# Expert rows added straight into the output by indirect DMA, in place of a combining stage

## The chip, the cores and the metric

The kernel runs on one core of one Trainium2 chip. The metric is the device time of one execution, in microseconds (us). Before the change the median of three runs is 3893.79 us (3890.04 to 3899.09). The profile is that of one execution more.

## The reference, cut to what matters

One layer of a decoder for 2048 prompt rows and 64 sample rows of width 1024. After two attention sublayers every row goes through a mixture of experts: a router picks two of 32 gated-MLP experts for it, and the weighted outputs of both are added to the row.

```python
def moe_ffn(xf, ids, wts, w_gate, w_up, w_down):
    ...
    xb = xf[row_tok].reshape(n_blocks, MOE_BLOCK, -1)      # MOE_BLOCK = 128
    def expert_block(args):
        xblk, e = args
        return (jax.nn.silu(xblk @ w_gate[e]) * (xblk @ w_up[e])) @ w_down[e]
    yb = lax.map(expert_block, (xb, blk_e)).reshape(rows, -1).astype(F32) * row_w[:, None]
    return jnp.zeros(xf.shape, F32).at[row_tok].add(yb).astype(xf.dtype)
# layer: h = h + MemCrossAttn(RMSNorm(h), mem);  y = h + HierMoE(RMSNorm(h))
```

## The kernel before, in words

The program is a list of stages (`STAGES`), one after the other; each ends with a barrier of all engines (`Stage.__exit__`). Inside a stage each engine has its own instruction queue, written out by hand, and semaphores order them. Four stages matter here.

**Memory attention** (`attend_memory`, L2507) walks over 17 tiles of 128 rows. SP stores the residual rows of a tile (`h2_store`, L2581) to the scratch tensor `h2`, and the normalised rows (`hn_store`) to `hn`.

**Routing** (`route`, L2784): DVE works out for each row its two experts, weights and places, in a list sorted by expert and padded to blocks of 128. Then POOL scatters the row numbers into the list `i_rows` (L2847): 34 indirect DMAs of 128 rows of 4 bytes. SP saves the places (`i_dst`), the weights and a plan: for each block its expert, the number of experts begun so far, and whether it begins a new one.

**Experts** (`experts`, L2945) loops over the blocks, two to a loop turn (`blocks`, L2980). The trace has 48 used blocks and 32 loads of each weight; the gate loads are some 19 us apart where an expert has one block and some 36.5 us where it has two: 16 experts of each kind. Each engine runs its `work` for block b:

- SP loads gate and up weights (2 MiB each) when a block begins a new expert.
- POOL waits until the rows of block b have been transposed, gathers the rows of block b+2 (`gather`, L3037, an indirect DMA of 128 rows of 4 KiB), loads the down weights (2 MiB) of block b+1 if that begins an expert, once DVE has split the down weights before them (`d_split`), waits for the gathered rows to land, and loads the row numbers of block b+4 (L3031).
- ACT takes the upper part of each weight (L3076), the SiLU, and copies the result of a block from PSUM to `ex_y` (L3107); it then stores `ex_y` to its place in the scratch tensor `yb` (L3109).
- DVE makes the lower part of each weight (L3130), splits the transposed rows (`ex_xT`, `ex_hT`) and multiplies (`ex_hh`).
- PE does three float32r products for each matmul (L136 to L138): up of block b, transposition of block b+2, gate of block b+1, down of block b.
- When the loop of SP is past the used blocks it stores zeros to the 18 unused blocks of `yb` (L3018).

**Combining** (`combine`, L3214): for each of 17 tiles, SP loads the `h2` rows, POOL gathers the two expert rows of each row from `yb` (L3254), DVE multiplies each by its weight and adds (L3264, L3269), SP stores the sum to `y` (L3231).

Of the kernel before, what the change touches and what calls it, by code (L numbers as in the profile page):

```python
# [53 lines left out]
NBX = NBLK + 4  # L54
# [2452 lines left out]
def attend_memory(nc, t, wo):  # L2507
# [6 lines left out]
    with Stage(nc, "mx") as s:  # L2514
# [27 lines left out]
                 "ox_turned oxT_hi oxT_ok xo_mm h1_in h2_ok ss_ok mean_ok root_ok rstd_ok h0_ok hn_ok h_turned hT_ok lg_mm lg_ok h2_out hn_out lg_out").split()  # L2542
# [16 lines left out]
        with nc.Block() as block:  # L2559
            @block.sync  # L2560
            def _(sp):
# [30 lines left out]
                sp.dma_start(wr[:], t["w_r"].rearrange("(k p) c -> p k c", p=P)).then_inc(E["w_in"], 16)  # L2592
                order(sp, lambda i: each((prompt(q_load), i + 1), (h1_load, i - 1), (h2_store, i - 2), (hn_store, i - 2),
                                         (sample_rows, i - 1), (lg_store, i - 3)))
                for e in ("h2_out", "hn_out", "lg_out"):
                    sp.wait_ge(E[e], NT * 16)

# [186 lines left out]
def route(nc, t):  # L2784
# [6 lines left out]
    with Stage(nc, "rt") as s:  # L2791
# [5 lines left out]
        tok = s.sb("tok", [P, NT], I32)  # L2797
        valid = s.sb("valid", [P, NT])
        zero = s.sb("zero", [P, NBX], I32)
# [21 lines left out]
        names = "loaded zero_ok zeroed own exp_ok sums_ok placed planned scattered saved".split()  # L2821
# [3 lines left out]
        with nc.Block() as block:  # L2825
            @block.sync
            def _(sp):
                sp.dma_start(lg[:], t["lg"].rearrange("n p c -> p n c")).then_inc(E["loaded"], 16)
                for dstt, name in ((io, "r_iota"), (kb, "r_blocks"), (ib, "r_places"), (tri, "r_tri"), (tok, "r_tok"), (valid, "r_valid")):
                    sp.dma_start(dstt[:], t[name]).then_inc(E["loaded"], 16)  # L2830
                sp.wait_ge(E["zero_ok"], 1)
                sp.dma_start(t["i_rows"].rearrange("(p n) o -> p (n o)", p=P), zero[:]).then_inc(E["zeroed"], 16)
                sp.wait_ge(E["placed"], 1)
                sp.wait_ge(E["planned"], 1)
                for dd, src in ((t["i_dst"], dsti[:]), (t["wts"], wts[:]), (t["i_plan"], plan[0:1])):
                    sp.dma_start(dd, src).then_inc(E["saved"], 16)
                sp.wait_ge(E["saved"], 48)

            @block.gpsimd
            def _(pool):  # L2840
                pool.memset(zero[:], 0).then_inc(E["zero_ok"], 1)
                pool.wait_ge(E["zeroed"], 16)
# [26 lines left out]
            def _(dve):  # L2869
# [75 lines left out]
def experts(nc, t):  # L2945
# [6 lines left out]
    with Stage(nc, "ex") as s:  # L2952
        ident = s.sb("ident", [P, P])
        plan = s.sb("plan", [1, 3, NBX + 1], I32)
        idx = s.sb("idx", [P, 2, 1], I32)
# [8 lines left out]
        zero = s.sb("zero", [P, D])  # L2964
# [5 lines left out]
                 "gate_mm up_mm sg_ok hh_ok h_turned h_hi h_ok y_mm y_ok y_out0 y_out1 zero_ok zero_out").split()  # L2970
# [9 lines left out]
        def blocks(eng, body, beyond=None):  # L2980

            used = read(eng, 0, NBX, NBLK)
            with eng.Fori(0, NBLK // 2) as i:
# [3 lines left out]
                if beyond:  # L2987
                    with eng.If(2 * i >= used):
                        for u in range(2):
                            beyond(2 * i + u)  # L2990
# [10 lines left out]
        with nc.Block() as block:  # L3001
            @block.sync
            def _(sp):
# [4 lines left out]
                def load(i, u, b):  # L3008
                    sp.sem_inc(E["zero_out"], 16)
# [10 lines left out]
                sp.wait_ge(E["zero_ok"], 1)  # L3020
                blocks(sp, load, nothing)
                sp.wait_ge(E["zero_out"], 16 * NBLK)

            @block.gpsimd
            def _(pool):
                pool.memset(zero[:], 0.0).then_inc(E["zero_ok"], 1)
# [6 lines left out]
                def gather(u, b, nth):  # L3033
# [3 lines left out]
                    pool.indirect_dma_start(xb[:, u, :], None, t["hn"].rearrange("n p d -> (n p) d"),  # L3037
                                            bass.IndirectOffsetOnAxis(ap=idx[:, u, :].bitcast(U32), axis=0)).then_inc(E[f"x_in{u}"], 16)
# [6 lines left out]
                for u in range(2):  # L3045
                    gather(u, u, 1)
# [3 lines left out]

                load_down(read(pool, 0, 0, NE - 1))

                def work(i, u, b):
                    pool.wait_ge(E["x_turned"], b + 1)
                    gather(u, b + 2, i + 2)
# [5 lines left out]
                    pool.wait_ge(E[f"x_in{u}"], 16 * i + 32)  # L3061
                    pool.sem_inc(E["seen"], 1)
                    load_rows(u, b + 4)

                pairs = blocks(pool, work)
                for u in range(2):
                    pool.wait_ge(E[f"idx_in{u}"], 16 * pairs + 32)

            @block.scalar
            def _(act):  # L3070
# [18 lines left out]
                def work(i, u, b):  # L3089
# [22 lines left out]
                for u in range(2):  # L3112
                    act.wait_ge(E[f"y_out{u}"], 16 * pairs + 16)
                    act.sem_inc(E["seen"], 1)

            @block.vector
            def _(dve):
# [5 lines left out]
                dve.sem_inc(E["y_out0"], 16)  # L3123
                dve.sem_inc(E["y_out1"], 16)
# [89 lines left out]
def combine(nc, t):  # L3214
    with Stage(nc, "cb") as s:
# [225 lines left out]
```

## Time and profile before

| | us |
|---|---|
| median of three runs | 3893.79 |
| the profiled execution | 3893.31 |
| its span in the trace | 3891.7 |
| PE busy over the span | 3223.6 (83%) |
| POOL busy over the span | 398.2 (10%) |

The span is what the trace covers; 1.6 us of the profiled execution's own time lie around it. Engines: PE is TensorE, DVE VectorE, ACT ScalarE, POOL GpSimd, SP the sync engine; a name with q is an engine's queue. A row of the timeline gives start, length, engine, line, operation, what is written and read, and in brackets how long the engine was idle before and what released it. "To landing" runs from the issue of a DMA until its data are there.

### The profile page before, as it was taken

Reading aid. Unit: us, or ns where it says so; the run is one execution under the profiler, and the core shown is the slowest. Engines: PE = TensorE matmul, PEld = TensorE weight load, DVE = VectorE, ACT = ScalarE, POOL = GpSimd, SP = SyncE. Lnnn points to the kernel's source line nnn. Section 1 sums busy time; section 2 is a strip of 40 time slices with the busy share of each in tenths; the row PEclk is TensorE's granted clock in tenths of the full one; section 3 lists DMA queues with packets and bytes.
Section 4 is the critical chain, followed back from the end, with each engine's and each line's share of the span. In section 5 each row is a group of like instructions: output and inputs, shape, how many; then the busy total and the mean of one; then the engine's idle time right before and its main releaser. Section 6 shows DMA issues by size and latency. Waiting matters only on the chain. (4 is left out here: it accounts for less than half of the span.)

```text
span 3891.7 us, 62377 instructions
## 1 busy us (share of the span) xinstructions
PE 3223.6 (83%) x22582; PEld 2700.3 (69%) x22583; DVE 1889.6 (49%) x2769; ACT 1486.6 (38%) x2958; POOL 398.2 (10%) x393
## 2 busy tenths in 40 slices
PE   7999999899969996568599966888339999999980
PEld 7999999788858885334277743677237778778860
DVE  5242356455534555311256631332436876686734
ACT  5112354355545554123123212443035655454520
POOL 1000000000000000040000010111131211121113
PEclk9999999899979998678699986988569999999995
DMA  4333332234441111164233322223158977796849
GB/s 163 121 110 140 140 110 99 86 115 127 148 127 35 64 56 51 51 200 135 98 117 114 115 95 89 90 95 98 37 193 305 340 283 269 273 350 228 293 180 340
DMA packets 309939, 591.64 MB, mean 152 GB/s; under 512 B 80597, under 2 KB 136323, under 8 KB 309230
## 3 DMA queue, kind: packets, MB, share of 16 engines
q1 hardware_dynamic: 250846, 365.54, 28.6%
q0 software_dynamic: 47776, 196.29, 13.7%
q10 hardware_dynamic: 11136, 27.27, 1.9%
q8 instruction: 130, 2.13, 0.2%
q14 instruction: 51, 0.42, 0.0%
HBM read 462.13 MB, written 160.44 MB: 160 GB/s over the span
## 5 line engine op out<-in xcount | busy, mean ns | idle before, releaser
L136 PE MATMUL pj_pu<-pj_w,pj_nT 128*128 128x256 f32 (+3 forms) x1088 | 306.8, 282 | 0.0
L137 PE MATMUL pj_pu<-pj_w,pj_nT 128*128 128x256 f32 (+3 forms) x1088 | 305.9, 281 | 0.0
L138 PE MATMUL pj_pu<-pj_w,pj_nT 128*128 128x256 f32 (+3 forms) x1088 | 305.2, 281 | 0.0
L137 PEld LDWEIGHTS pj_pu<-pj_w,pj_nT 128*128 128x128 f32 (+1 forms) x1088 | 202.1, 186 | 0.0
L138 PEld LDWEIGHTS pj_pu<-pj_w,pj_nT 128*128 128x128 f32 (+1 forms) x1088 | 202.0, 186 | 0.0
L136 PEld LDWEIGHTS pj_pu<-pj_w,pj_nT 128*128 128x128 f32 (+1 forms) x1088 | 201.6, 185 | 0.1
L3076 ACT ACTIVATE ex_gate<-ex_gate_raw 128x2048 fp32r<-128x2048 f32 x64 | 119.1, 1909 | 204.0 <-DMA ex_gate_raw<-in_w_gate 116.8
L716 ACT ACTIVATE att_prob<-att_score,att_res 128x256 f32<-128x256 f32 (+1 forms) x384 | 127.6, 443 | 143.9 <-DVE att_res L752 143.9
L3130 DVE TENSOR_TENSOR ex_gate<-ex_gate_raw,ex_gate 128x2048 fp32r<-128x2048 f32 x64 | 143.8, 2288 | 72.1 <-ACT ex_gate L3076 60.9
L136 PE MATMUL pj_pu<-pj_nT,pj_w 128*128 128x384 f32 (+2 forms) x480 | 175.3, 365 | 0.0
L136 PE MATMUL ex_py<-ex_down,ex_hT 128*128 128x512 f32 x384 | 152.7, 398 | 26.2 <-DVE ex_hT L131 26.2
L138 PE MATMUL pj_pu<-pj_nT,pj_w 128*128 128x384 f32 (+2 forms) x480 | 170.2, 355 | 0.0
L758 DVE COPY att_pT<-att_turn 128x512 f32<-128x512 f32 (+1 forms) x192 | 107.2, 572 | 129.9 <-PE att_turn L812 129.4
L137 PE MATMUL pj_pu<-pj_nT,pj_w 128*128 128x384 f32 (+2 forms) x480 | 169.9, 354 | 0.0
L136 PE MATMUL ex_gu<-ex_gate,ex_xT 128*128 128x512 f32 x392 | 162.9, 416 | 0.4 <-DVE ex_gate L3130 0.4
L826 PE MATMUL att_outp<-att_va,att_pT 128*128 128x65 f32 x1200 | 160.5, 271 | 0.3 <-DVE att_pT L758 0.3
L3130 DVE TENSOR_TENSOR ex_up<-ex_up_raw,ex_up 128x2048 fp32r<-128x2048 f32 x64 | 143.8, 2288 | 28.7 <-issue 22.7
L826 PEld LDWEIGHTS att_outp<-att_va,att_pT 128*128 128x128 f32 x1200 | 148.9, 191 | 11.7 <-issue 8.0
L138 PE MATMUL ex_gu<-ex_gate,ex_xT 128*128 128x512 f32 x392 | 154.4, 394 | 0.0
L137 PE MATMUL ex_gu<-ex_gate,ex_xT 128*128 128x512 f32 x392 | 153.7, 392 | 0.0
L3130 DVE TENSOR_TENSOR ex_down<-ex_down_raw,ex_down 128x2048 fp32r<-128x2048 f32 x64 | 143.7, 2287 | 15.5 <-issue 10.7
L138 PE MATMUL ex_py<-ex_down,ex_hT 128*128 128x512 f32 x384 | 149.7, 390 | 0.0
(580 smaller groups left out, 8168.6 us busy)
## 6 DMA issues: line engine op xcount, KB each, us to landing
ex_gate_raw<-in_w_gate SPq DMA_DIRECT2D x32, 2048.0 KB
ex_up_raw<-in_w_up SPq DMA_DIRECT2D x32, 2048.0 KB, 11.2
ex_down_raw<-in_w_down POOLq DMA_DIRECT2D x32, 2048.0 KB, 8.4
tmp_yb<-ex_y ACTq DMA_DIRECT2D x48, 512.0 KB, 7.1
out_win_k<-in_cache_k POOLq DMA_DIRECT2D x8, 2032.0 KB, 13.1
out_win_v<-in_cache_v POOLq DMA_DIRECT2D x8, 2032.0 KB, 14.2
tmp_att<-att_res POOLq DMA_DIRECT2D x48, 264.0 KB, 4.4
pout_att<-tmp_att SPq DMA_DIRECT2D x16, 792.0 KB, 7.4
```

Of the source, the lines that this page charges most:

```text
L136: pe.matmul(out, ah, bh, start=start, stop=False)
L137: pe.matmul(out, ah, bl, start=False, stop=False)
L138: return pe.matmul(out, al, bh, start=False, stop=stop)
L716: e = act.activation(prob[:, b % 2, h, lo:], score[:, place(h), lo:], ACT.Exp, bias=res[:, b % RES, AH * VA + h:AH * VA + h + 1])
L758: dve.tensor_copy(pT[:, j, 0:n, :], turn[:, j % 2, 0:n * P].rearrange("p (c n) -> p c n", c=n)).then_inc(p_moved, 1)
L826: last = pe.matmul(outp[:, j // 2, (2 * (j % 2) + h) * VA:(2 * (j % 2) + h + 1) * VA], pT[:, j, h * halves + k, :], va[:, slot, 2 * j + h, :],
L3076: act.activation(half[p][:, 0, part(p, h)], raw[p][:, part(p, h)], ACT.Copy).then_inc(E[p + "_hi"], 1)
L3130: dve.tensor_tensor(half[p][:, 1, part(p, h)], raw[p][:, part(p, h)], half[p][:, 0, part(p, h)].bitcast(F32), ALU.subtract).then_inc(E[p + ...
```

## The change

Memory attention stores its residual rows into the output `y` itself; `h2`, `yb`, `i_dst` and the saved weights are gone. The list `i_rows` now holds pairs (row number, weight), padded with rows of an extra tile at the end of `hn` and `y` (the former padding was row 0), which memory attention fills once. The experts' ACT multiplies by the weight in the copy from PSUM. POOL then adds the 128 rows of `ex_y` to their rows of `y` by an indirect DMA with an add, and waits until that has landed before it goes on. Gathers run three blocks ahead instead of two. ACT's store to `yb`, the zeros, and the whole combining stage are taken out.

```diff
-NBX = NBLK + 4
+NBX = NBLK + 8
...
-                    sp.dma_start(t["h2"][i], h2[:]).then_inc(E["h2_out"], 16)
+                    sp.dma_start(t["y"][i], h2[:]).then_inc(E["h2_out"], 16)
...
+                sp.wait_ge(E["consts_in"], 80)
+                for n in ("hn", "y"):
+                    sp.dma_start(t[n][NT], gf[:]).then_inc(E["spare_out"], 16)
...
-        tok = s.sb("tok", [P, NT], I32)
+        tokw = s.sb("tokw", [P, 2, NT, 2], I32)
...
+                sp.dma_start(t["i_rows"].rearrange("(p n) o -> p (n o)", p=P), t["r_fill"]).then_inc(E["filled"], 16)
...
-                for dd, src in ((t["i_dst"], dsti[:]), (t["wts"], wts[:]), (t["i_plan"], plan[0:1])):
-                    sp.dma_start(dd, src).then_inc(E["saved"], 16)
-                sp.wait_ge(E["saved"], 48)
+                sp.dma_start(t["i_plan"], plan[0:1]).then_inc(E["saved"], 16)
+                sp.wait_ge(E["saved"], 16)
 
...
-                                                tok[0:n, i:i + 1], None).then_inc(E["scattered"], 16)
+                                                tokw[0:n, a, i, :], None).then_inc(E["scattered"], 16)
...
+                own.then(dve.tensor_copy(tokw[:, :, :, 1].bitcast(F32), wts[:]))
...
-        idx = s.sb("idx", [P, 2, 1], I32)
+        idx = s.sb("idx", [P, 2, 2], I32)
+        place = s.sb("place", [P, 2, 2], I32)
...
-                def nothing(b):
-                    sp.dma_start(t["yb"][b], zero[:]).then_inc(E["zero_out"], 16)
-
-                sp.wait_ge(E["zero_ok"], 1)
-                blocks(sp, load, nothing)
-                sp.wait_ge(E["zero_out"], 16 * NBLK)
+                blocks(sp, load)
...
+                def load_place(u, b):
+                    pool.dma_start(place[:, u, :], rows[b]).then_inc(E[f"place_in{u}"], 16)
+
+                def gather(u, nth):
...
-                    gather(u, u, 1)
+                    gather(u, 1)
+                load_place(0, 0)
+                load_down(read(pool, 0, 0, NE - 1))
                 for u in range(2):
                     pool.wait_ge(E[f"x_in{u}"], 16)
                     load_rows(u, 2 + u)
-
-                load_down(read(pool, 0, 0, NE - 1))
+                pool.wait_ge(E["x_turned"], 1)
+                gather(0, 2)
+                pool.wait_ge(E["x_in0"], 32)
+                load_rows(0, 4)
...
                 def work(i, u, b):
-                    pool.wait_ge(E["x_turned"], b + 1)
-                    gather(u, b + 2, i + 2)
+                    v = 1 - u
+                    pool.wait_ge(E["x_turned"], b + 2)
+                    gather(v, i + 2 + u)
                     with pool.If(read(pool, 2, b + 1, 1)):
                         e = read(pool, 0, b + 1, NE - 1)
                         pool.wait_ge(E["d_split"], 2 * began(pool, b + 1))
                         pool.sem_inc(E["seen"], 1)
                         load_down(e)
-                    pool.wait_ge(E[f"x_in{u}"], 16 * i + 32)
+                    pool.wait_ge(E[f"x_in{v}"], 16 * i + 32 + 16 * u)
                     pool.sem_inc(E["seen"], 1)
-                    load_rows(u, b + 4)
+                    load_rows(v, b + 5)
+                    load_place(v, b + 1)
+                    pool.wait_ge(E["y_ok"], 2 * b + 4)
+                    pool.sem_inc(E["seen"], 1)
+                    pool.indirect_dma_start(t["y"].rearrange("n p d -> (n p) d"), bass.IndirectOffsetOnAxis(ap=place[:, u, 0:1].bitcast(U32), axis=0),
+                                            y[:, u, :], None, compute_op=ALU.add).then_inc(E["added"], 16)
+                    pool.wait_ge(E["added"], 16 * b + 16)
+                    pool.sem_inc(E["y_free"], 1)
 
                 pairs = blocks(pool, work)
                 for u in range(2):
-                    pool.wait_ge(E[f"idx_in{u}"], 16 * pairs + 32)
+                    pool.wait_ge(E[f"idx_in{u}"], 16 * pairs + 32 + 16 * (1 - u))
+                    pool.wait_ge(E[f"place_in{u}"], 16 * pairs + 16 * (1 - u))
...
                     act.wait_ge(E["y_mm"], b + 2)
-                    act.wait_ge(E[f"y_out{u}"], i * 16 + 16)
+                    act.wait_ge(E["y_free"], b + 1)
+                    act.wait_ge(E[f"place_in{u}"], 16 * i + 16)
+                    act.sem_inc(E["seen"], 1)
                     for n in range(2):
-                        act.activation(y[:, u, 512 * n:512 * n + 512], py[:, n, :], ACT.Copy).then_inc(E["y_ok"], 1)
-                    act.wait_ge(E["y_ok"], 2 * b + 4)
-                    act.dma_start(t["yb"][b], y[:, u, :]).then_inc(E[f"y_out{u}"], 16)
-
-                pairs = blocks(act, work)
-                for u in range(2):
-                    act.wait_ge(E[f"y_out{u}"], 16 * pairs + 16)
-                    act.sem_inc(E["seen"], 1)
+                        act.activation(y[:, u, 512 * n:512 * n + 512], py[:, n, :], ACT.Copy, scale=place[:, u, 1:2].bitcast(F32)).then_inc(E["y_ok"], 1)
+
+                blocks(act, work)
...
-def combine(nc, t):
...
-                sp.dma_start(di[:], t["i_dst"]).then_inc(consts_in, 16)
...
-                    sp.dma_start(h[0:n, u, :], t["h2"][i, 0:n]).then_inc(h_in[u], 16)
...
-                    for a, dst, sem in ((0, a1, a_in), (1, a2, b_in)):
-                        pool.indirect_dma_start(dst[0:n, u, :], None, yb,
-                                                bass.IndirectOffsetOnAxis(ap=di[0:n, a, i:i + 1].bitcast(U32), axis=0)).then_inc(sem[u], 16)
...
-                    dve.scalar_tensor_tensor(out=s1[0:n, u, :], in0=a1[0:n, u, :], scalar=w[0:n, 0, i:i + 1], in1=h[0:n, u, :],
...
-                    dve.scalar_tensor_tensor(out=s2[0:n, u, :], in0=a2[0:n, u, :], scalar=w[0:n, 1, i:i + 1], in1=s1[0:n, u, :],
-                                             op0=ALU.mult, op1=ALU.add).then_inc(both_ok, 1)
...
-          memory_attention, route, experts, combine]
+          memory_attention, route, experts]
...
+        "r_fill": np.ascontiguousarray(np.stack([ROWS + np.arange(NBX * BLK) % P, np.zeros(NBX * BLK)], 1).reshape(P, -1).astype(np.int32)),
...
-    "i_rows": (NBX * BLK, 1), "i_dst": (P, 2, NT), "wts": (P, 2, NT), "i_plan": (1, 3, NBX + 1), "yb": (NBLK, P, D),
+    "i_rows": (NBX * BLK, 2), "i_plan": (1, 3, NBX + 1),
...
-    "y": (NT, P, D), "mem_kp": (NMEM // P, P, XW), "mem_vp": (NMEM // P, P, XW),
```

Two places in the queue of POOL show what moves. The first is the end of a block's work in the experts' loop, up to the gather of the next block's work; `ex_idx` are row numbers to gather by, `ex_place` those to add at, `ex_xb` gathered rows, the ISA rows are semaphore steps. Before:

```order
L3061 ISA
L3031 ISA
L3031 DMA ex_idx<-tmp_i_rows 128x1
L3054 REGISTER_ALU
L3037 DMA ex_xb<-tmp_hn,ex_idx 128x1024
L2975 ISA
L2975 TENSOR_LOAD ex_plan
```

With the change:

```order
L3058 ISA
L3020 ISA
L3020 DMA ex_idx<-tmp_i_rows 128x2
L3023 ISA
L3023 DMA ex_place<-tmp_i_rows 128x2
L3062 ISA
L3064 DMA out_y<-ex_y,ex_place 2304x1024
L3066 ISA
L3051 REGISTER_ALU
L3026 ISA
L3029 DMA ex_xb<-tmp_hn,ex_idx 128x1024
```

A load of places and the adding DMA, with a wait before it and one behind it, now stand between the load of row numbers and the next gather.

The second place is the start of the experts' stage on POOL, ahead of the loop. Before:

```order
L3031 DMA ex_idx<-tmp_i_rows 128x1 x2
L3037 DMA ex_xb<-tmp_hn,ex_idx 128x1024 x2
L3031 DMA ex_idx<-tmp_i_rows 128x1 x2
L2975 TENSOR_LOAD ex_plan
L2975 ISA x2
L3041 ISA
L3041 DMA ex_down_raw<-in_w_down 128x4x1024
```

With the change:

```order
L3020 DMA ex_idx<-tmp_i_rows 128x2 x2
L3029 DMA ex_xb<-tmp_hn,ex_idx 128x1024 x2
L3023 DMA ex_place<-tmp_i_rows 128x2
L2975 TENSOR_LOAD ex_plan
L2975 ISA x2
L3033 ISA
L3033 DMA ex_down_raw<-in_w_down 128x4x1024
L3020 DMA ex_idx<-tmp_i_rows 128x2 x2
L3029 DMA ex_xb<-tmp_hn,ex_idx 128x1024
L3020 DMA ex_idx<-tmp_i_rows 128x2
```

The first down weights are now loaded ahead of the wait for the gathered rows, and a third gather stands ahead of the loop.

## Rows read from the trace of the kernel before

**Rows 1.** The page: the span.

```profile
span 3891.7 us, 62377 instructions
```

**Rows 2.** Busy time by stretch: routing, experts' loop, combining (columns: stretch, length, busy PE PEld DVE ACT POOL, clock, DMA share, GB/s).

```profile
2768.00:2857.00 89.00, 4.45 (x8) 2.27 (x8) 37.38 (x75) 1.76 (x3) 37.45 (x36) 0.50 0.05 7
2911.00:3781.00 870.00, 841.76 (x3947) 689.41 (x3945) 614.99 (x419) 443.20 (x346) 129.92 (x123) 1.00 0.79 282
3788.00:3891.00 103.00, 0.00 (x0) 0.00 (x0) 43.66 (x34) 0.00 (x0) 33.27 (x34) 0.50 0.92 336
```

**Rows 3.** The chain that ended last: its last piece (start, length, what).

```profile
3886.62 1.28 DVE cb_s L3269
```

**Rows 4.** Timeline of ACT: the copies of a block's result, in mid-loop and of the last block.

```profile
3170.80 1.09 ACT L3107 ACTIVATE ex_y<-ex_py 128x512 f32<-128x512 f32 x2 [1.47 <-PE ex_py L138]
...
3779.82 1.09 ACT L3107 ACTIVATE ex_y<-ex_py 128x512 f32<-128x512 f32 x2 [15.32 <-PE ex_py L138]
```

**Rows 5.** Timeline of SP: gate loads of one-block experts, then of two-block experts.

```profile
3066.54 0.38 SPq L3015 DMA_DIRECT2D ex_gate_raw<-in_w_gate  x1
...
3085.47 0.38 SPq L3015 DMA_DIRECT2D ex_gate_raw<-in_w_gate  x1
...
3525.61 0.38 SPq L3015 DMA_DIRECT2D ex_gate_raw<-in_w_gate  x1
...
3562.18 0.38 SPq L3015 DMA_DIRECT2D ex_gate_raw<-in_w_gate  x1
```

**Rows 6.** Busy time by stretch: one-block experts, then a two-block expert (columns as in rows 2).

```profile
3020.00:3105.00 85.00, 80.65 (x379) 65.64 (x378) 74.58 (x49) 55.73 (x42) 16.89 (x13) 1.00 0.98 363
...
3562.00:3599.00 37.00, 36.14 (x171) 29.77 (x170) 22.34 (x17) 15.80 (x13) 3.84 (x5) 1.00 0.67 230
```

**Rows 7.** Timeline of POOL in the experts' loop.

```profile
3113.11 0.99 POOL L3037 DMA_INDIRECT ex_xb<-tmp_hn,ex_idx  x1 [0.33 <-issue]
3120.57 0.56 POOL L3031 DMA_DIRECT2D ex_idx<-tmp_i_rows  x1 [6.47 <-DMA ex_xb<-tmp_hn,ex_idx]
...
3147.22 0.54 POOL L3031 DMA_DIRECT2D ex_idx<-tmp_i_rows  x1
3148.09 0.99 POOL L3037 DMA_INDIRECT ex_xb<-tmp_hn,ex_idx  x1 [0.33 <-issue]
3182.96 0.77 POOL L3041 DMA_DIRECT2D ex_down_raw<-in_w_down  x1 [33.88 <-DVE ex_down L3130]
...
3184.97 2.54 POOL L3037 DMA_INDIRECT ex_xb<-tmp_hn,ex_idx  x1 [0.70 <-issue]
...
3203.54 3.02 POOL L3037 DMA_INDIRECT ex_xb<-tmp_hn,ex_idx  x1 [0.33 <-issue]
```

**Rows 8.** Timeline of DVE beside the last of those rows: splitting of the up weights.

```profile
3203.41 4.50 DVE L3130 TENSOR_TENSOR ex_up<-ex_up_raw,ex_up 128x2048 fp32r<-128x2048 f32 x2 [0.95 <-ACT ex_up L3076]
```

**Rows 9.** The tile `ex_xb`: landing of the 50 gathers.

```profile
DMA to landing us min/median/max: 5.1/6.7/10.4
```

**Rows 10.** The tile `ex_y`: landing of the 48 plain stores to `yb`.

```profile
DMA to landing us min/median/max: 2.6/7.1/8.5
```

**Rows 11.** Waits in the experts' loop (who, for what: us in total, times, longest).

```profile
POOL ex_down_raw L3041 <- DVE ex_down L3130: 535.1, 30, 33.9
...
ACT ex_down L3076 <- DMA ex_down_raw<-in_w_down: 5.7, 6, 1.0
```

**Rows 12.** Timeline at the start of the experts' stage: second gather, first down load, first gate weights.

```profile
2862.56 0.98 POOL L3037 DMA_INDIRECT ex_xb<-tmp_hn,ex_idx  x1 [0.30 <-issue]
...
2871.12 0.57 POOL L3031 DMA_DIRECT2D ex_idx<-tmp_i_rows  x1 [3.17 <-DMA ex_xb<-tmp_hn,ex_idx]
2872.60 0.77 POOL L3041 DMA_DIRECT2D ex_down_raw<-in_w_down  x1 [0.92 <-issue]
...
2872.99 3.71 ACT L3076 ACTIVATE ex_gate<-ex_gate_raw 128x2048 fp32r<-128x2048 f32 x2 [85.90 <-DMA ex_gate_raw<-in_w_gate]
```

**Rows 13.** Timeline of routing: DVE's copy of the places.

```profile
2803.73 0.18 DVE L2928 CAST rt_dsti<-rt_dst 128x34 int32<-128x34 f32 x1
```

**Rows 14.** Timeline of SP at the start of memory attention.

```profile
2409.09 0.43 SPq L2592 DMA_DIRECT2D mx_wr<-in_w_r  x1
2417.57 0.33 SPq L2568 DMA_DIRECT2D mx_q<-tmp_qx  x1
```

More of the change, by code:

```diff
@@ L2541, in attend_memory @@
         names = ("consts_in w_in km_mm kT_ok q_in q_turned qT_ok score_ok max_ok exp_ok p_turned pT_ok pv_ok rden_ok ox_ok ox_in "
[L2542 removed]
+                 "ox_turned oxT_hi oxT_ok xo_mm h1_in h2_ok ss_ok mean_ok root_ok rstd_ok h0_ok hn_ok h_turned hT_ok lg_mm lg_ok h2_out hn_out lg_out spare_out").split()
         E = dict(zip(names, s.sem(*names)))
@@ L2820, in route @@
         pt = s.ps("total", [P, 2, 512])
-        names = "loaded zero_ok zeroed own exp_ok sums_ok placed planned scattered saved".split()
+        names = "loaded filled own exp_ok sums_ok placed planned scattered saved".split()
         E = dict(zip(names, s.sem(*names)))
@@ L2969, in experts @@
         names = ("consts_in seen idx_in0 idx_in1 x_in0 x_in1 g_in u_in d_in g_hi u_hi d_hi g_split u_split d_split x_turned x_hi x_ok "
-                 "gate_mm up_mm sg_ok hh_ok h_turned h_hi h_ok y_mm y_ok y_out0 y_out1 zero_ok zero_out").split()
+                 "gate_mm up_mm sg_ok hh_ok h_turned h_hi h_ok y_mm y_ok place_in0 place_in1 added y_free").split()
         E = dict(zip(names, s.sem(*names)))
@@ L2978, in began, with blocks @@
             return read(eng, 1, b, NE)
-        def blocks(eng, body, beyond=None):
+        def blocks(eng, body):
             used = read(eng, 0, NBX, NBLK)
@@ L3210, in _ @@
                 blocks(pe, work)
-def combine(nc, t):
-    with Stage(nc, "cb") as s:
-        di = s.sb("di", [P, 2, NT], I32)
-        w = s.sb("w", [P, 2, NT])
-        h = s.sb("h", [P, 2, D])
-        a1 = s.sb("a1", [P, 2, D])
-        a2 = s.sb("a2", [P, 2, D])
-        s1 = s.sb("s1", [P, 2, D])
-        s2 = s.sb("s2", [P, 2, D])
-        consts_in, first_ok, both_ok = s.sem("consts_in", "first_ok", "both_ok")
-        h_in, a_in, b_in, out_ok = (s.sem(n + "0", n + "1") for n in ("h_in", "a_in", "b_in", "out_ok"))
-        rows_of = lambda i: P if i < PT else NS
-        yb = t["yb"].rearrange("n p d -> (n p) d")
-        with nc.Block() as block:
-            def store(sp, i):
-                n = rows_of(i)
-                sp.wait_ge(both_ok, i + 1)
-                sp.dma_start(t["y"][i, 0:n], s2[0:n, i % 2, :]).then_inc(out_ok[i % 2], 16)
-            @block.sync
-            def _(sp):
-                sp.dma_start(di[:], t["i_dst"]).then_inc(consts_in, 16)
-                sp.dma_start(w[:], t["wts"]).then_inc(consts_in, 16)
-                for i in range(NT):
-                    n, u = rows_of(i), i % 2
-                    need(sp, first_ok, i - 1)
-                    sp.dma_start(h[0:n, u, :], t["h2"][i, 0:n]).then_inc(h_in[u], 16)
-                    if i:
-                        store(sp, i - 1)
-                store(sp, NT - 1)
-                for u in range(2):
-                    sp.wait_ge(out_ok[u], 16 * ((NT + 1 - u) // 2))
-            @block.gpsimd
-            def _(pool):
-                pool.wait_ge(consts_in, 32)
-                for i in range(NT):
-                    n, u = rows_of(i), i % 2
-                    need(pool, both_ok, i - 1)
-                    for a, dst, sem in ((0, a1, a_in), (1, a2, b_in)):
-                        pool.indirect_dma_start(dst[0:n, u, :], None, yb,
-                                                bass.IndirectOffsetOnAxis(ap=di[0:n, a, i:i + 1].bitcast(U32), axis=0)).then_inc(sem[u], 16)
-            @block.vector
-            def _(dve):
-                dve.wait_ge(consts_in, 32)
-                for i in range(NT):
-                    n, u = rows_of(i), i % 2
-                    dve.wait_ge(h_in[u], 16 * (i // 2) + 16)
-                    dve.wait_ge(a_in[u], 16 * (i // 2) + 16)
-                    dve.scalar_tensor_tensor(out=s1[0:n, u, :], in0=a1[0:n, u, :], scalar=w[0:n, 0, i:i + 1], in1=h[0:n, u, :],
-                                             op0=ALU.mult, op1=ALU.add).then_inc(first_ok, 1)
-                    dve.wait_ge(first_ok, i + 1)
-                    dve.wait_ge(b_in[u], 16 * (i // 2) + 16)
-                    need(dve, out_ok[u], 16 * (i // 2))
-                    dve.scalar_tensor_tensor(out=s2[0:n, u, :], in0=a2[0:n, u, :], scalar=w[0:n, 1, i:i + 1], in1=s1[0:n, u, :],
-                                             op0=ALU.mult, op1=ALU.add).then_inc(both_ok, 1)
@@ L3433 @@
     out = {n: r[f"out_{n}"] for n in OUTPUTS}
-    flat = {n: out[n].reshape((ROWS, -1)) for n in ("k", "v", "y")}
+    flat = {n: out[n].reshape((-1, out[n].shape[-1])) for n in ("k", "v", "y")}
     return (flat["y"][:SEQ].reshape(1, SEQ, D), flat["y"][SEQ:SEQ + NS].reshape(DEC_B, DEC_T, D),
```

28 lines of the change are left out of this document (8 added, 20 removed).

## The prediction

> **What bounds the kernel now.** I read the head of the page first, for the span [rows 1], then busy time by stretch [rows 2]. The reader is to see three regimes there: routing is short DVE steps and a queue of POOL scatters; the experts' loop is TensorE, 841.8 of 870 us busy at the granted clock 1.00, with the DMA engines at 0.79; combining has neither TensorE nor ScalarE, and the DMA engines are 0.92 busy at 336 GB/s. The chain that ended last [rows 3] ends in combining's last add. A barrier stands ahead of combining, so nothing hides it: what is removed there is worth its whole length. The price has to be looked for in the experts' loop, and there the overall TensorE share says little; what counts is whether POOL, which issues little today, can keep to TensorE's pace with one more DMA that it waits for.
>
> The pace comes from SP's gate loads [rows 5]. Experts of one block follow each other at 3085.47 - 3066.54 = 18.93 us. Experts of two blocks come at 3562.18 - 3525.61 = 36.57, or 18.28 a block. There are 16 of each kind, so 16 and 32 blocks. One-block stretches hold the DMA engines at 0.98 busy and 363 GB/s, two-block stretches at 0.67 and 230 [rows 6].
>
> **The change, part by part**
>
> *Combining is gone.* From the end of the last copy out of PSUM (3779.82 + 1.09 = 3780.9 [rows 4]) to the end of the span, 110.8 us pass [rows 1]. In their place comes the last add alone: some 0.3 to wake POOL, a landing that I take as a quiet gather's 5.1 [rows 9] and 1.3 more for the second read, and 0.7 to leave the stage: 7.4. Gain 103.4. The plain store that is also gone is part of the 110.8.
>
> *The experts' loop, POOL's own circle.* This is the term that decides. Before, POOL mostly sat waiting for the split of down weights (535 us in 30 waits [rows 11]); its gathers, loads of row numbers and down loads had time to spare. Now each block's work on POOL is one serial chain: gather, wait for it to land, two loads of row numbers and places, the add, wait for it to land, next gather. Nothing in it overlaps, because the engine itself waits. From rows 7: from a gather's start to the load of row numbers behind its landing, 3120.57 - 3113.11 = 7.46; that load's slot, 3148.09 - 3147.22 = 0.87, now twice, 1.74; the step from one block's work to the next, 0.33 to 0.70, say 0.5. That is 9.7 us and the landing L of the add.
>
> L is in no row. From below: a gather moves the same 128 rows of 4 KiB through the same queue and does less, 5.1 at the least and 6.7 in the median [rows 9]; a plain store of the block went down to 2.6 when quiet [rows 10]. From above: two gathers one after the other, 13.4. An add must read the old row before it can write, so I take a median gather and one quiet transfer of the same size behind it: 6.7 + 2.6 = 9.3. It is nearer to the gather, since issue, queue and row count are those of a gather.
>
> In a two-block stretch the circle is then 9.7 + 9.3 = 19.0, against 18.28: +0.72 x 32 = 23 us. In a one-block stretch POOL's issue itself is longer, 2.54 and 3.02 instead of 0.99 [rows 7], beside DVE's splitting of weights [rows 8]; the add is issued right behind the copy from PSUM, where DVE splits the next gate weights. With 1.8 more the circle is 20.8, against 18.93: +1.87 x 16 = 30. Together +53. For any L the two make 48 L - 393.5 us while both are positive, so a microsecond of landing is worth 48. The price falls away below about 7.4.
>
> *The down load behind the add.* The load for block b+2 now waits for the add of block b. It was issued 3182.96 - 3171.89 = 11.1 us after a copy from PSUM [rows 4, 7]. Now it comes 0.3 + 9.3 and some 2.6 (a gather's issue and three reads of the plan) after one: 12.2, or 1.1 later. ScalarE waited for these weights in 6 of 30 cases, by 1.0 at most [rows 11], so the others have room: 0, already inside the circle's loss. Where L is above some 10, it is this load that is late next, then ScalarE's upper half, DVE's lower half, and TensorE's down matmul.
>
> *Traffic.* An add reads 0.5 MB more than the store it replaces: 1.4 us of DMA time a block at 363 GB/s [rows 6]. In one-block stretches that is under the 1.87 counted already; in two-block ones a third of the engines' time is free. The 18 zero stores near the end ran beside the last blocks: 0. Padding rows are gathered from 128 rows instead of one, the same bytes: 0.
>
> *The start of the stage.* The first down load moves from 2872.60 to about 2865.5, behind the second gather's issue (2863.5), a load of places and a read. The first gate weights land at 2872.99, and the queue that the down load joins holds gathers until 2871.1 [rows 12]. So the two overlap for about 2 us and share the engines: +1.0. If they shared from the start, +3; if not at all, 0.
>
> *Routing.* One more copy of 34 numbers ahead of the places, the like of which takes 0.18 [rows 13]: +0.3 with its wait. The scatters keep their count and rows (8 bytes instead of 4), the plan is hidden behind them, the two saved tables were too.
>
> *Memory attention.* Residual rows go to another tensor, in the same store. Two stores of 0.5 MB fill the spare tile once; SP issues them between 2409.09 and its next load at 2417.57 [rows 14], 8 us in which it has nothing to issue: 0, at worst the 2.6 of one quiet transfer. ScalarE's copy gains a scale and keeps its shape: 0. It loses its wait and the store's issue: 0, since it isn't the bound.
>
> *Sum.* Against the profiled execution's 3893.3 (0.5 below the median of the runs): -103.4 + 53 + 1.0 + 0.3 = -49.1, or **3844**.
>
> **The rivals**
>
> *The add is hidden.* If L stays below 7.4, a little more than the median gather, POOL keeps pace in both kinds of stretch and only the fixed terms remain: 3893.3 - 102.1 = 3791. For it: two-block stretches leave a third of the DMA time free, and the gather now runs three blocks ahead and goes out ahead of the down load instead of behind it, so it may land sooner than 7.46. Against it: an add that is scarcely longer than a gather has no row behind it. Chance 0.20.
>
> *The add moves its data twice over, and POOL becomes the bound.* If everything in a gather beyond the 1.0 of issue doubles, L = 1.0 + 2 x 5.7 = 12.4 and the loop loses 48 x 12.4 - 393.5 = 202: 3993. It turns slower than before where the loss passes 102.1, at L = 10.3, only 1.0 above my value. For it: POOL's chain has no slack, and in one-block stretches the DMA engines are full. Against it: the quiet gather's 5.1 is mostly fixed, and a fixed part need not double. Chance of L above 10.4, slower than before: 0.34; of these 0.10 lie above 12.4, up to 4041 with the two gathers' 13.4.
>
> The Trainium skill speaks for this rival: in "Collectives: The Full Stack", section "The bandwidth ceiling", a reducing DMA is slower "because the add needs two source reads", both on one ring, and runs at about half the rate of a copy. By that rule the sum would be this rival's 3993. No row of this trace has an adding DMA, so neither agreement nor disagreement is shown.
>
> *No change to speak of.* Gain and loss cancel for L between about 10.1 and 10.4: 0.06.
>
> **How the numbers follow.** My forecast, L from 7.4 to 10.1 and so 3791 to 3885, has 0.40; with the hidden add, faster has 0.60. Within 0.2% (7.8 us, about what a measurement of this kernel can tell from no change) has 0.06, slower 0.34. The predicted time is the likeliest case's. The faster cases alone would give 3790 to 3885; as slower has a third, the range reaches up to the doubled transfer, 3993, and leaves out the 0.10 above it and little below.
>
> **What would show it.** Right: no combining; an add that lands in 8 to 10 us; POOL's circle at 19 us in two-block and near 21 in one-block stretches, TensorE waiting some 50 us more in the loop, for gathered rows or for down weights. Hidden: gate loads still 18.3 and 18.9 apart, and POOL waiting for the copy from PSUM. Doubled: an add of 12 us or more, gate loads 44 us apart in two-block stretches, the down load named as releaser. I would be wrong altogether if the pace of the loop changed without POOL's circle being its length, for instance because gate weights come late.

## The result, and the profile after

The changed kernel takes 3960.11 us (median of 4 runs, 3951.88 to 3986.01), beside 3896.44 for the kernel before (4 runs): a ratio of 1.0173, 95% interval 1.0121 to 1.0226. **It is slower**, by 1.7%: inside the range of the prediction, but on the other side of its forecast. The profiled execution took 3964.36, 71.1 more than that of before (3893.31). The page of after, its span and its fourth part, the chain that ended last:

```profile
span 3962.8 us, 62343 instructions
...
DMA 12%; PE 6%; issue 3%; DVE 2%; ACT 2%; POOLq 1%; ACTq 0%; POOL 0%; SPq 0%; DVEq 0%
DMA ex_down_raw<-in_w_down 7%; DMA out_y<-ex_y,ex_place 5%; PE ex_py L136 2%; PE ex_py L137 2%; PE ex_py L138 2%; DVE ex_down L3131 1%; ACT ex_down L3081 1%; POOLq L2975 1%; ACT ex_y L3114 0%; DVE ex_hT L131 0%; PE ex_gu L138 0%; PE ex_gu L136 0%; PE ex_gu L137 0%; DMA ex_gate_raw<-in_w_gate 0%; DVE ex_hT L129 0%
```

The two largest links are the load of down weights and the add. The 71.1 us split at two rows of ScalarE's timeline, the first and the last copy out of PSUM (the last against [rows 4]; before, the first began at 2910.85):

```profile
2911.16 1.27 ACT L3114 ACTIVATE ex_y<-ex_py,ex_place 128x512 f32<-128x512 f32 x2
...
3945.54 1.27 ACT L3114 ACTIVATE ex_y<-ex_py,ex_place 128x512 f32<-128x512 f32 x2 [15.86 <-PE ex_py L138]
3948.59 1.66 POOL L3064 DMA_INDIRECT out_y<-ex_y,ex_place  x1 [5.00 <-issue]
```

- Ahead of the first copy: 2911.16 - 2910.85 = +0.3.
- The loop, first to last copy: 3945.54 - 2911.16 = 1034.4, against 3779.82 - 2910.85 = 869.0: **+165.4**.
- From the end of the last copy (3946.81) to the end of the span: 16.0, against 110.8: **-94.8**. (The copy itself is 0.2 longer.)

So combining was worth what the prediction said, less 8.6, and the loop lost three times its 53. Busy time by stretch: the whole loop, to be read against the second line of [rows 2], and two neighbouring stretches that the chain below explains (columns as there):

```profile
2911.00:3947.00 1036.00, 883.38 (x3948) 719.63 (x3946) 616.49 (x419) 447.39 (x347) 260.15 (x218) 0.93 0.71 228
3182.00:3197.00 15.00, 14.93 (x72) 12.11 (x71) 4.45 (x4) 2.61 (x4) 3.62 (x5) 1.00 0.91 281
3197.00:3212.00 15.00, 7.86 (x28) 6.35 (x29) 12.73 (x8) 6.89 (x5) 2.95 (x3) 0.77 0.34 104
```

The loop has as many matmul records as before (3948 and 3947), but TensorE idles for 1036 - 883.4 = 152.6 us instead of 870 - 841.8 = 28.2, and its busy time is 41.6 longer. The first is three quarters of the loss, the second, a clock granted at 0.93 instead of 1.00, one quarter.

What TensorE idles for stands in the waits of the loop (who, for what: us in total, times, longest):

```profile
POOL ex_xb L3029 <- issue: 436.2, 47, 12.3
...
ACT ex_down L3081 <- DMA ex_down_raw<-in_w_down: 191.0, 24, 12.9
...
DVE ex_down L3131 <- ACT ex_down L3081: 144.1, 29, 10.6
PE ex_py L136 <- DVE ex_hT L131: 141.5, 32, 8.5
POOL out_y L3064 <- ACT ex_y L3114: 138.0, 29, 8.6
```

ScalarE's wait for down weights has gone from 5.7 us [rows 11] to 191.0; through DVE it becomes TensorE's wait ahead of the down matmul. The first row is POOL ahead of a gather, where it waits for an add to land, 47 times (the profile writes this wait as "issue"). The last row says that POOL is also early: in 29 of the 48 blocks it waited for the copy out of PSUM. An engine whose own circle sets the pace would not do that.

The chain in one cycle of 44.4 us, two blocks (start, length, what):

```profile
3167.75 0.69 ACT ex_y L3114
...
3169.31 9.50 DMA out_y<-ex_y,ex_place
...
3180.15 0.30 POOLq L2975
...
3182.89 13.24 DMA ex_down_raw<-in_w_down
3196.15 1.92 ACT ex_down L3081
...
3200.30 2.28 DVE ex_down L3131
...
3204.14 0.79 PE ex_py L136
3204.93 0.43 PE ex_py L137
...
3212.15 0.69 ACT ex_y L3114
...
3213.72 9.30 DMA out_y<-ex_y,ex_place
...
3227.10 13.74 DMA ex_down_raw<-in_w_down
```

Copy, add, landing of the add, POOL's gather and reads of the plan, down load, its landing, the split on ScalarE and DVE, the down matmul, copy. The load lies on this path because POOL, which issues it, stands behind the add. It also lands late: 13.2 and 13.7 us, where the median before was 8.4. In the first of the two stretches above the DMA engines are 0.91 busy: the up weights of the expert go out 0.53 us behind the down load, and the next add 4.8 us behind it. POOL, SP and ScalarE in that cycle, from their timelines:

```profile
3169.31 1.67 POOL L3064 DMA_INDIRECT out_y<-ex_y,ex_place  x1 [7.23 <-ACT ex_y L3114]
3180.29 1.79 POOL L3029 DMA_INDIRECT ex_xb<-tmp_hn,ex_idx  x1 [9.30 <-issue]
3182.89 0.78 POOL L3033 DMA_DIRECT2D ex_down_raw<-in_w_down  x1 [0.81 <-issue]
...
3183.42 0.37 SPq L3010 DMA_DIRECT2D ex_up_raw<-in_w_up  x1
...
3187.73 1.67 POOL L3064 DMA_INDIRECT out_y<-ex_y,ex_place  x1 [0.37 <-issue]
...
3196.15 3.71 ACT L3081 ACTIVATE ex_down<-ex_down_raw 128x2048 fp32r<-128x2048 f32 x2 [9.49 <-DMA ex_down_raw<-in_w_down]
...
3213.72 1.67 POOL L3064 DMA_INDIRECT out_y<-ex_y,ex_place  x1 [5.08 <-ACT ex_y L3114]
```

From issue to use, then, the down load has 3196.15 - 3182.89 = 13.3 us, and ScalarE stands idle for the last 9.5 of them. Now three new rows of the kernel **before**: a down load on POOL, issued while an expert of two blocks is worked on, the copy of the first of these two blocks, and the use of the load on ScalarE:

```profile
3220.77 0.76 POOL L3041 DMA_DIRECT2D ex_down_raw<-in_w_down  x1 [4.78 <-DVE ex_down L3130]
...
3227.35 1.09 ACT L3107 ACTIVATE ex_y<-ex_py 128x512 f32<-128x512 f32 x2 [2.75 <-PE ex_py L138]
...
3248.40 3.72 ACT L3076 ACTIVATE ex_down<-ex_down_raw 128x2048 fp32r<-128x2048 f32 x2 [0.96 <-issue]
```

There it had 27.6. Of the 32 down loads before, 15 were issued 24 to 28 us ahead of their use, the other 17, in one-block stretches, 8 to 11 us ahead. After, 31 of 32 have 8 to 15 us. As the use now waits for the load, this lead hides how late the load is; the prediction measured it against a copy. Before, it went out 7.7 us ahead of the end of that copy (3227.35 + 1.09 - 3220.77). With the change, in the cycle above, it goes out 14.4 us behind the end of the corresponding copy (3167.75 + 0.69 = 3168.44). Over the 14 such loads of each timeline the medians are 7.7 ahead and 14.3 behind; in one-block stretches they are 11.1 behind before and 17.4 after. **In two-block stretches the change delayed this load by some 22 us, and in one-block stretches by 6, not by 1.1.**

### The profile page after: what moved, and what is told of

It reads as the page before. It is cut to its first block and busy times, and to the rows that moved or that the text cites. A ratio compares the mean times of both kernels' runs of the same rounds, so it can differ in the third digit from the quotient of the medians.

```text
span 3962.8 us, 62343 instructions
## 1 busy us (share of the span) xinstructions
PE 3256.8 (82%) x22538; PEld 2728.6 (69%) x22583; DVE 1843.2 (47%) x2736; ACT 1490.8 (38%) x2958; POOL 497.0 (13%) x456
## 5 line engine op out<-in xcount | busy, mean ns | idle before, releaser
L136 PE MATMUL ex_py<-ex_down,ex_hT 128*128 128x512 f32 x384 | 169.3, 441 | 141.5 <-DVE ex_hT L131 141.5
L136 PEld LDWEIGHTS ex_py<-ex_down,ex_hT 128*128 128x128 f32 x384 | 81.2, 211 | 172.1 <-issue 154.8
L3081 ACT ACTIVATE ex_down<-ex_down_raw 128x2048 fp32r<-128x2048 f32 x64 | 118.8, 1905 | 191.0 <-DMA ex_down_raw<-in_w_down 191.0
L3114 ACT ACTIVATE ex_y<-ex_py,ex_place 128x512 f32<-128x512 f32 x96 | 60.8, 684 | 286.9 <-PE ex_py L138 286.8
L136 PE MATMUL ex_gu<-ex_gate,ex_xT 128*128 128x512 f32 x392 | 163.8, 418 | 2.2 <-issue 1.1
L137 PE MATMUL ex_py<-ex_down,ex_hT 128*128 128x512 f32 x384 | 163.6, 426 | 0.0
L138 PE MATMUL ex_py<-ex_down,ex_hT 128*128 128x512 f32 x384 | 162.4, 423 | 0.0
## 6 DMA issues: line engine op xcount, KB each, us to landing
out_win_v<-in_cache_v POOLq DMA_DIRECT2D x8, 2032.0 KB, 14.4
```

What stands on the lines that cost most here:

```text
L136: pe.matmul(out, ah, bh, start=start, stop=False)
L137: pe.matmul(out, ah, bl, start=False, stop=False)
L138: return pe.matmul(out, al, bh, start=False, stop=stop)
L3081: act.activation(half[p][:, 0, part(p, h)], raw[p][:, part(p, h)], ACT.Copy).then_inc(E[p + "_hi"], 1)
```

## The experiments

Three theories. **A**: the down load, queued on POOL behind the add's landing, reaches ScalarE too late. **B**: POOL's own circle (gather, landing, row numbers and places, add, landing) is longer than a block; this is the prediction's term. **C**: the add's traffic slows the weight loads. "Loop" below is always from the start of the first copy to that of the last, in the profiled execution: 869.0 before, 1034.4 with the change. It is one execution of each kernel, and these lie up to 11 us from the median of their runs (e2: 3834.99 beside 3845.83), so a difference of two loops is good to some 10 us.

**e1_down_from_sp.** SP issues the down loads, so nothing of the weights is behind the add.

```diff
 # SP, block b
+                    with sp.If(read(sp, 2, b + 1, 1)):
+                        fetch("g", "w_gate", b + 1)
+                    with sp.If(read(sp, 2, b, 1)):
+                        fetch("d", "w_down", b)
+                    with sp.If(read(sp, 2, b + 1, 1)):
+                        fetch("u", "w_up", b + 1)
...
 # POOL, block b
-                    with pool.If(read(pool, 2, b + 1, 1)):
-                        e = read(pool, 0, b + 1, NE - 1)
-                        pool.wait_ge(E["d_split"], 2 * began(pool, b + 1))
-                        load_down(e)
```

> The down weights are issued by SP, between the gate and the up weights, instead of by POOL behind the wait for the add; the add and POOL's wait for its landing stay. Theory A (the down load queued behind the landing of the add is the loss: add, down load, ScalarE, VectorE, TensorE, copy, add is one chain of 44 us for two blocks): the loop from the first to the last copy out of PSUM falls from 1035 us to 870 to 890, time 3800 to 3820. Theory B (the forecast's: POOL's own circle of gather, loads and add, 19 to 21 us a block, sets the pace, with or without the down load): the loop falls to 915 to 960 at best, time 3850 to 3890. Theory C (the add's reading and writing slows the weight loads): the down load still takes 13 us to land and the loop stays above 1000, time above 3930.

The runs of the kernel before beside this and the next three experiments have a median of 3896.28 us (19 runs), beside the last two, on another chip, 3897.81 (7 runs). Measured: 3877.85 us (10 runs), ratio to before 0.9956 [0.9934, 0.9978]; 82 us under the change, loop 957.1. ScalarE's wait for down weights falls from 191.0 us to 0.8. TensorE now waits for gathered rows, ahead of their transposition, and around experts of one block the chain runs through POOL alone for several blocks on end. Waits, then that chain:

```profile
PEld ex_tr L3170 <- issue: 82.8, 26, 5.5
...
PE ex_tr L3170 <- DMA ex_xb<-tmp_hn,ex_idx: 71.9, 26, 5.1
```

```profile
3307.82 5.71 DMA ex_xb<-tmp_hn,ex_idx
...
3315.74 12.47 DMA out_y<-ex_y,ex_place
...
3329.27 8.60 DMA ex_xb<-tmp_hn,ex_idx
...
3341.14 11.95 DMA out_y<-ex_y,ex_place
...
3354.56 7.14 DMA ex_xb<-tmp_hn,ex_idx
```

That is B's circle: 3329.27 - 3307.82 = 21.5 and 25.3 us. The time missed what A alone expected (3800 to 3820) by 58 us and lies in B's range. But 77.3 us went from the loop while POOL's wait for the add stayed where it was, and with them the wait of ScalarE. So A held the time of the changed kernel, and B lies right under it. C is not the cause of the loss as a whole: the add and its traffic are all still there. The edit also sets the order of the three loads in SP's queue; e2, which leaves that queue alone, gains more.

**e2_wait_later.** POOL waits for an add only in the next block's work, behind that block's gather, down load and row numbers. It takes both the down load and the gather out from behind the add.

```diff
                     load_rows(v, b + 5)
+                    pool.wait_ge(E["added"], 16 * b + 16)
+                    pool.sem_inc(E["y_free"], 1)
                     load_place(v, b + 1)
...
                                             y[:, u, :], None, compute_op=ALU.add).then_inc(E["added"], 16)
-                    pool.wait_ge(E["added"], 16 * b + 16)
-                    pool.sem_inc(E["y_free"], 1)
```

> POOL waits for the landing of an add only when the next block's gather, down load and row numbers are through, ahead of the next add; the down load stays in POOL's queue. Theory A: the down load goes out some 10 us earlier after each copy, the chain loses the add's 9.5 us, 34 to 35 us for two blocks, less than TensorE needs: loop 870 to 890, time 3800 to 3820. Theory B: the circle loses most of the landing too, so the same 3800 to 3820; this run does not tell A from B. Theory C: 3930 or more.

Measured: 3845.83 us (4 runs), ratio 0.9893 [0.9868, 0.9918]; 114 us under the change, loop 903.6. (The first wait of that kind is met by a spare load of places, the last one stands behind the loop.) ScalarE's waits in the loop:

```profile
ACT ex_gate L3083 <- DMA ex_gate_raw<-in_w_gate: 103.3, 15, 9.3
...
ACT ex_down L3083 <- DMA ex_down_raw<-in_w_down: 18.9, 11, 4.0
```

The wait, not the add, cost the most: 130.8 of the loop's 165.4 us. As the edit frees two things at once it does not part A from B. Both expected 3800 to 3820, so 26 us are missing. The waits show a rest: gate weights are waited for now.

**e3_plain_scatter.** The indirect DMA stores instead of adding; all waits stay.

```diff
-                                            y[:, u, :], None, compute_op=ALU.add).then_inc(E["added"], 16)
+                                            y[:, u, :], None).then_inc(E["added"], 16)
```

> The add's DMA without its add: the rows of a block are written over the rows of y, so the sum over the two experts and the residual is left out; every wait stays. Theory A: only the landing's shortening counts, once for two blocks: if it lands 2 to 3 us sooner (7 to 8 us), 24 x 2.5 = 60 us less, time 3890 to 3915. Theory B: once a block, 3830 to 3860. Theory C: the down load lands in 8 to 9 us as before the change and the loop is back at 870 to 890, time 3800 to 3820.

Measured: 3883.79 us (10 runs), ratio 0.9962 [0.9938, 0.9985]; 76 us under the change, loop 955.8. The scatter's line and the landing of `ex_y`, with the add first, then without (duration in ns, least/median/most):

```profile
L3064 POOL DMA_INDIRECT out_y<-ex_y,ex_place x48: 1656/1678/3769, 2913.3 to 3948.6; - x48
...
DMA to landing us min/median/max: 6.2/9.9/13.2
```

```profile
L3064 POOL DMA_INDIRECT out_y<-ex_y,ex_place x48: 1013/1014/3113, 2920.0 to 3877.6; - x48
...
DMA to landing us min/median/max: 3.4/8.1/11.4
```

In this arrangement an add takes 0.7 us more to issue and lands 1.8 later than a store, both counted from the start of the issue, so the 0.7 is part of the 1.8. If only this length counted, once for each down load behind the first as in A's chain, the loop would lose 31 x 1.8 = 56 us; it lost 78.6. The time, 3883.79, is 6 us below A's range and 24 above B's. The rest is not parted: without the add the down load itself is faster too, 10.7 us from issue to use in two-block stretches instead of 13.1 (medians of 14 loads). ScalarE still waits 115.1 us for down weights, in 22 waits, so A is eased and not gone. As the edit takes away length and traffic together, this run does not part A from C; what the traffic costs with A and B out of the way, e5 shows.

**e4_both.** e1 and e2 together: SP issues the down loads, and POOL waits for an add one block later.

```diff
 # POOL, block b
-                        load_down(e)
...
                     load_rows(v, b + 5)
+                    pool.wait_ge(E["added"], 16 * b + 16)
```

> Both edits at once: down weights issued by SP, and the add's landing waited for only ahead of the next add. Theory A: nothing more to gain than in either alone, within 10 us of the better one, 3795 to 3815. Theory B: faster than the down weights from SP alone by 40 us or more, since only here and with the later wait the circle is short. Theory C: 3930 or more.

Measured: 3828.38 us (4 runs), ratio 0.9844 [0.9818, 0.9869]; loop 900.2. **This beats both kernels**, the one before by 1.6%. Against e1 it takes away POOL's wait alone, and that gives back 49.5 us of the median and 56.9 of the loop. B expected 40 or more: it is B's circle, at a size that the prediction's +53 had. A alone expected no more than 3815, so it is not the whole account. Busy time of the loop, and two of its waits:

```profile
2907.00:3809.00 902.00, 849.91 (x3949) 696.76 (x3947) 616.53 (x419) 446.33 (x347) 198.55 (x188) 0.99 0.80 262
```

```profile
POOL out_y L3066 <- ACT ex_y L3115: 285.3, 45, 17.3
...
ACT ex_gate L3082 <- DMA ex_gate_raw<-in_w_gate: 81.8, 14, 7.3
```

The clock is back at 0.99, and POOL waits for the copy in 45 of 48 blocks: it has slack again. The loop is still 31.2 longer than before the change.

**e5_both_plain.** e4 with e3's edit: is that rest the add's traffic? Against e4:

```diff
-                                            y[:, u, :], None, compute_op=ALU.add).then_inc(E["added"], 16)
+                                            y[:, u, :], None).then_inc(E["added"], 16)
```

> SP issues the down loads, POOL waits for the scatter's landing only in the next block's work, and the indirect DMA stores without adding (the add is left out, so the sums of the experts are missing). It asks what the loop of e4_both still lacks (900.8 us from the first to the last copy out of PSUM, 869.0 before the change). Theory traffic (the add's read of 0.5 MB a block, 24 MB over 48 blocks, some 67 us of DMA time at 363 GB/s, delays the weight loads): without it the loop comes down by 20 to 32 us, to 869 to 881, and the median to 3796 to 3808. Theory order (the weight loads come late because all three stand in SP's one queue, whatever the add reads): the loop stays within 8 us of 900.8, the median between 3820 and 3836.

Measured: 3808.57 us (4 runs), ratio 0.9774 [0.9758, 0.979]; loop 882.5.

```profile
2914.00:3799.00 885.00, 841.50 (x3949) 690.03 (x3947) 616.33 (x419) 446.66 (x347) 179.03 (x188) 1.00 0.74 267
...
ACT ex_gate L3082 <- DMA ex_gate_raw<-in_w_gate: 76.6, 15, 6.6
```

The loop falls by 17.7 and the median by 19.8, to within 2 us of what the traffic theory allowed at the most. The DMA engines' busy time says what the add costs them: 0.80 x 902 - 0.74 x 885 = 67 us, 1.4 a block. So about 18 of the 31 us are the add's traffic and issue. The other 13.5 stay: ScalarE waits for gate weights as long as in e4, and since e2, whose SP loads no down weights, has such a wait too (103.3 us), SP's order is not shown to be its cause. One rival was not tried: the copy with its scale takes 0.18 us longer in each block (1.27 and 1.09), 8.6 us of ScalarE over the loop. And 13.5 us are little more than the scatter of single executions.

**e6_sp_plain.** e1 with e3's edit: the circle stays, shorter. Against e1:

```diff
-                                            y[:, u, :], None, compute_op=ALU.add).then_inc(E["added"], 16)
+                                            y[:, u, :], None).then_inc(E["added"], 16)
```

> SP issues the down loads, POOL waits right behind the indirect DMA, and that stores without adding (the add is left out, so the sums of the experts are missing). Theory B (once the down load is out of POOL's queue, POOL's serial circle of gather, landing, two loads of numbers, add, landing sets the pace): the circle loses the add's extra issue and landing, 0.7 and some 0.9 to 1.8 us, in each of 48 blocks: 77 to 120 us below e1_down_from_sp's 3878 if the circle bound in every block, down to e4_both's 3828 at the least, where other limits begin, so 3790 to 3830. Theory A alone (only the down load behind the add mattered, and e1_down_from_sp has taken all of that): no more than 15 us below e1_down_from_sp, 3863 to 3880.

Measured: 3818.13 us (4 runs), ratio 0.9808 [0.9789, 0.9827]; loop 888.6, and 59.7 us under e1. TensorE's wait for gathered rows falls from 71.9 to:

```profile
PE ex_tr L3170 <- DMA ex_xb<-tmp_hn,ex_idx: 11.0, 8, 2.5
```

B again. The circle loses 1.6 us of landing (medians 7.4 and 9.0, the shorter issue included), 1.6 x 48 = 77 if it bound in every block; the loop lost 68.5. The time is in B's range; A alone expected 15 us at the most.

## Why the prediction was right or wrong

The loop's +165.4 us can be laid out by what each edit takes off it, in this order: the down load out from behind the add (1034.4 to 957.1) 77.3; POOL's wait (to 900.2) 56.9; the add itself (to 882.5) 17.7; the rest against 869.0, 13.5. In another order the shares differ. POOL's wait first (e2) takes 130.8, and the down load then only 3.4 more (17.5 of the median, e2 against e4); without the add first, 78.6 go at once (e3). The down load and the gather stand behind the same wait, and what is freed first has the larger share.

- **Combining is gone: right**, short of its size. -94.8 instead of -103.4. The last add was issued 1.8 us after the copy instead of 0.3, and landed in 6.2 (6.4 was forecast). Between that landing, 3948.59 + 6.2 = 3954.8, and the end of the span lie 8.0 us in which the timeline shows no work on any engine, where the prediction had 0.7. The trace has POOL's rows for them, which the timeline leaves out: after its wait for the last add POOL still goes through the loop's nine turns for the 18 unused blocks, 4.2 us of branches (3954.86 to 3959.03), and then a drain (L2997) takes 2.4 us. In e2, where the wait stands behind the loop, the same turns run while the last add lands, and 3.7 us are left.
- **POOL's own circle: right in kind and size, but it was not what set the pace.** L was taken as 9.3 and came out at 9.9. In the cycle above POOL's two circles take 3213.72 - 3169.31 = 44.4 us, of which it waits 5.1 for the copy, so 39.3; twice 19.0 was forecast. In e1, around two experts of one block, one circle takes 21.5 and 25.3 instead of 20.8. The +53 shows up as 56.9, but only once the down load is out of the way, and in another order the share is another; that the sizes agree so closely is partly luck. In the kernel as changed, POOL waited for the copy in 29 blocks.
- **"The down load behind the add ... 0": the step that failed.** It was worth 77.3 with POOL's wait in place (e1), and it turned the sign. Three readings went wrong. The rows it was measured on, 3182.96 in [rows 7] and the copy in [rows 4], are of one-block experts, where the load comes 11.1 us behind a copy. In two-block stretches, some two thirds of the blocks, it had gone out 7.7 us ahead of that copy's end and 27.6 ahead of its use. Moved to 12.2 behind the copy it is there not 1.1 but 19.9 us later, with 7.7 us left to its use, less than the 8.4 that it took to land; it came 14.3 behind. Then the landing was taken as it was, while the new moment of issue puts the load beside the up load and ahead of the next add: 13.2 instead of 8.4. And a longest wait of 1.0 us in 6 of 30 cases [rows 11] was read as room in all; it said that these 6 had none.
- **"Where L is above some 10, it is this load that is late next"**: the mechanism was named, at the wrong threshold. In the cycle above it binds with L at 9.5 and 9.3.
- **The clock was in no term.** In the cycle above TensorE idles for 7.2 us, and of the down matmuls behind that the first takes 0.79 us and the next six 0.43 each, instead of 0.23, with the granted clock at 0.50, the 1.2 GHz level, from 3202 to 3205. Over the loop TensorE's busy time is 41.6 us longer, and 36.6 of these are in the down matmuls (303.8 and 267.2).
- **Start, routing, memory attention, traffic**: the start came out at +0.3 with everything ahead of it, +1.3 forecast. The add's 1.4 us of DMA time a block was right (67 / 48), but it was not free: up to 18 us in the loop, where 0 was written for it beside the circle's loss. "16 of each kind" is not what the copies show: 17 experts have one block, 14 have two and the last has three; by that the +53 would be 54. For L at 10.1 the prediction's own formula gives 3882.5 and not 3885.
- **The rivals.** "Doubled" gave 3993 and the result is 33 us below it, but not by its mechanism: the add did not reach 12.4 us in the median. That the range holds the result is luck; slower had been given 0.34. Two of the three signs set down for this rival came true all the same, gate loads 44 us apart (3167.28 and 3211.70) and the down load as releaser. They were signs of A and did not belong to the length of the add. What came true is the sign of being wrong altogether: the pace changed without POOL's circle being its length, though for the down weights and not the gate weights. In landings the adds are not twice as long: 9.9 beside 8.1, 9.0 beside 7.4, 8.4 beside 7.1 us in the median, add and store of the same block in the same arrangement; the shortest are 6.2 beside 3.4. In the time of the DMA engines they take twice as long: a packet of 4 KiB of the last block takes 328 ns with the add and 159 without (medians of 128, the changed kernel and e3). The Trainium skill's rule ("Collectives: The Full Stack", "The bandwidth ceiling"), half the rate because an add reads two sources, agrees with the packets and not with the landings. The down load that goes out 0.53 us ahead of the up load lands in 13.2 us instead of 8.4. This agrees with the Trainium skill, "DMA: Bandwidth & Descriptors", "Queues, rings and completion order", which has each DMA engine take packets from its queue rows in turn.

## What to carry to other kernels

Before a wait is put on an engine's queue, list what else that queue issues, and for each such transfer read the time from issue to use in every regime of the loop; a prefetch that is early in one regime and just in time in another has no single slack. Here the cure was to keep the add and move the wait: let the queue go on and wait for the landing one block later, ahead of the next add, and issue weights from a queue that never waits for results. And here a stall of TensorE cost more than its length: behind 7.2 idle us the next matmuls ran at a granted clock of 0.50.

## What was not expected of the hardware

- An indirect DMA that adds took POOL 1.68 us to issue where the plain one took 1.01 (128 rows of 4 KiB, medians of 48); the slowest took 3.77 and 3.11. The first packet of the last block moved 2.2 us after the start of the issue with the add and 1.6 without.
- The price of the add depends on what stands behind it: the same replacement by a store was worth 76 us in the changed kernel, 60 with the down loads on SP, and 20 with the wait moved as well.
- After 7.2 us without matmuls (3196.9 to 3204.1) TensorE went on at a granted clock of 0.50, and had 1.00 again from 3208 on. Busy time of these stretches of the changed kernel, columns as in [rows 2]:

```profile
3198.00:3202.00 4.00, 0.00 (x0) 0.00 (x0) 3.91 (x2) 4.00 (x4) 0.34 (x1) 0.82 0.58 200
3202.00:3205.00 3.00, 0.86 (x2) 0.77 (x3) 2.75 (x4) 1.46 (x1) 1.47 (x1) 0.50 0.27 49
3205.00:3208.00 3.00, 3.00 (x9) 2.32 (x9) 2.56 (x3) 0.00 (x0) 0.52 (x1) 0.60 0.33 126
3208.00:3212.00 4.00, 4.00 (x19) 3.26 (x19) 3.52 (x2) 0.43 (x1) 0.62 (x2) 1.00 0.02 1
```
